# Later fetches, earlier stores and a small planning allowance for first-stage products in a hybrid decoder step whose order a planner writes

## The chip, the cores and the metric

The kernel runs on the 8 cores of one Trainium2 chip. Each core handles one prompt of 2048 tokens and 16 sample tokens, with its own copy of all weights; the cores exchange nothing. The time of an execution is that of its slowest core, in microseconds (us) on the device. The times shown are medians over runs. Engines are named as in the profile: PE (matmul), PEld (its weight loads), DVE (vector), ACT (activation), POOL (GpSimd, which also issues the weight loads on DMA queue q0) and SP (which issues nearly all other transfers, on queue q1).

## The reference, cut to what matters

```python
def layer(x, pool_prev, ...):
    h = rmsnorm(x, g_mix)
    proj = h @ w_in
    a, z = proj[..., :o1], gelu(proj[..., o1:o2])
    gate_a, gate_b = sigmoid(proj[..., o2:o3]), sigmoid(proj[..., o3:])
    pa = pool_mixer(seq_a, ...)              # trailing means of 2, 4, 8, 16 rows, then a 128x128 product
    sg, v = spatial_gating(z, w_s, b_s, g_v) # u * (causal 128x128 mixing of rmsnorm(v) + b_s)
    merged = gate_a * (pa @ w_pool_out) + gate_b * (sg @ w_gmlp_out)
    x = x + merged @ w_out
    h2 = rmsnorm(x, g_ffn)
    x = x + (silu(h2 @ w_gate) * (h2 @ w_up)) @ w_down
    return x, new_pool, v                    # and rmsnorm(x, g_final) is the output
```

Model width is 1024, the FFN has 2816 columns (22 slices of 128), weights arrive as float32 and are cast to float16 by the transfer.

## The kernel before, in words

The program is not written as five instruction streams. Every operation is put on a list by `Prog.add` with an assumed duration, a priority and what it reads and writes, and `Prog.schedule` (L258) plays the list through a model of the five engines, the eight PSUM banks and two DMA queues (`Rings`). Each engine takes next the operation that can start earliest; among equals the one of lowest priority number. The order in which operations were taken is then the order in which each engine issues them on the chip; only the order is kept, not the times. `Prog.resolve` adds the semaphore waits. So an assumed time matters only where it changes an order, and an engine whose next operation is late on the chip stands still though a later one could run.

`slack` is a number added in the model to the moment an operation may start: for a matmul, `schedule` adds it to the moment its operands from other engines are done (L294) and its bank is free (L282). `mm` (L549) gives it 200 ns (`PEM`) for the products after the first stage (priority over 900) and none for those of the first stage. For a DMA the slack is added to its assumed landing.

The stages, in order of time on core 3:

* First stage (to about 121 us): the 16 tiles of 128 rows of x are loaded by SP, normed, transposed on PE (`norm`), and multiplied with the a, v and u parts of w_in. Where the planned order leaves PE idle for over 0.7 us early on, dummy matmuls (L1446) are put in. The row `b_s` is fetched by ACT's queue (`bs_row`, L661) and spread over 128 partitions by a float32 matmul against ones (`spread`, L691).
* Gates and merge (to about 269 us): the gate products in a Strassen-like form with 344 columns (`product`), with weights in three slots `Rg` filled by POOL (`ring_load`, L993: two loads of 256 KB, then four DVE sums on them).
* The product with w_out (to about 331 us): the loop over `wo_order` (L1202), 17 steps n_ = 0 to 16: sixteen tiles of 128 prompt rows, and the 16 sample rows (NT) at n_ = 6. For each prompt tile x is fetched again (`xload`), 16 matmuls of 512 columns fill two banks, DVE adds them to x, ACT and POOL work out the row norm, ACT scales into one of four buffers `hb` (tile `Sx` in the trace), DVE multiplies by the gain, and SP issues a transposing DMA into `hT` (the sample rows are transposed by PE instead). Tiles n_ = 0 to 5 live in `X`; n_ = 7 to 16 in rows 0 to 9 of `Pr`, so they have to be stored to `xd` in DRAM (`xstore`, L1198) before the FFN writes its row f into row f of `Pr`.
* FFN, two groups of 10 and 12 slices: f = 0, 1, 2 run together over the three blocks of 344 columns, then f = 3, 4, 5, 6 one after the other. The weights of f go to slot f % 3 of `Rg`: those of f = 3, 4 and 5 can be fetched only as f = 0, 1 and 2 let their slot go. Then the down projection of each group (`down_pair`), which fetches x from `xd`, adds, and stores it, to `yp` after the last norm.

The orders that the diff touches: the fetches of n_ = 7 to 16 all wait for one thing, that the fetch of prompt tile 10 has landed (`x_dma[10]`). The stores of n_ = 7, 8, 9 follow their own tile's norm; those of n_ = 10 and 11 wait for the last norm of the stage (`tlast`, the landing of its transposing DMA); those of n_ = 12 to 16 wait until the weights of f = 3 have landed (`Bf[3]['ld']`).

Of the kernel before, what the change touches and what calls it, by code (L numbers as in the profile page):

```python
# [34 lines left out]
PEM = 200.0  # L35
# [10 lines left out]
C_BS = 136  # L46
# [386 lines left out]
def nfree(ap):  # L433
    n = 1
    for (_, c) in list(ap.ap)[1:]:
        n *= int(c)
    return n


def build_nc():  # L440
    nc = bass.Bass("TRN2", target_bir_lowering=False, dynamic_dma_scratch_size=4096)

    def din(name, shape):
        return nc.dram_tensor(name, list(shape), F32, kind="ExternalInput").ap()
# [7 lines left out]
    cst = din("cst", [128, C_ALL])  # L452
# [11 lines left out]
    with es:  # L464
# [63 lines left out]
        bs_row = wsb[:, 0:512]  # L528
# [20 lines left out]
        def mm(pt, sl, pairs, prio, start=True, stop=True, after=(), more=False):  # L549
            out = PV(pt, sl)  # L550
            n = nfree(pairs[0][1])
            rd = [x for pr in pairs for x in pr]

            def fn(e):
                ap = P.r(out)
                ins = None
                for i, (l, rr) in enumerate(pairs):
                    ins = e.matmul(out=ap, lhsT=l, rhs=rr, start=(start and i == 0),  # L558
                                   stop=(stop and i == len(pairs) - 1), skip_group_check=more)
                return ins  # L560
            f = 4.0 if pairs[0][1].dtype == F32 else 1.0
            per = max(25.0, n / 2.4 * f + 2.5)
            o_ = P.add('pe', fn, reads=rd, writes=[out], dur=per * len(pairs), lat=140.0, prio=prio, after=after)
            o_.slack = PEM if prio > 900 else 0.0
            return o_

        def pe_multi(pt, items, prio, per, reads, nmm):
# [50 lines left out]
        def rows(n, b):  # L618
            return (max(1.0, n / 16.0), 45.0 + b * 0.04)

        def dma(q, out, in_, sem, nbytes, prio, after=(), tr=False):
            def fn(e):
                if tr:
                    return e.dma_start_transpose(out=out, in_=in_)
                return e.dma_start(out=out, in_=in_)  # L625
            return P.add(q, fn, reads=[in_], writes=[out],
                         dur=(570.0 if q == 'pool' else 450.0), lat=0.0, prio=prio, dma=sem, nbytes=nbytes,
                         after=after, margin=(300.0 if q == 'pool' else 0.0))
# [19 lines left out]
        x_dma = {}  # L648

        def xload(t, prio, after=()):  # L650
            s_ = xtile(t)
            if t < NT:
                o_ = dma('sp', slots[s_][:, 0:D], xp[t * 128:(t + 1) * 128, :], 'x%d' % s_, rows(128, 4096), prio, after)
            else:
                o_ = dma('sp', slots[s_][:NSMP, 0:D], xs[:, :], 'x%d' % s_, rows(16, 4096), prio, after)
            x_dma[t] = o_
# [1 line left out]
        on = memset('dve', ones[0:1, :], 1.0, -9.0)  # L658
        xload(0, -10.0)
        dma('act', idg[:, :], cst[:, C_ID:C_ID + 136], 'c0', rows(128, 544), -9.9)  # L660
        dma('act', bs_row[0:1, :], cst[0:1, C_BS:C_BS + 512], 'c4', rows(1, 2048), -9.8)  # L661
        for t in range(1, NXS):
            xload(t, -10.0 + 0.1 * t)
        wd_ = {}
# [470 lines left out]
        for p in range(4):  # L1135
# [10 lines left out]
            if p == 0:  # L1146
                for k in range(4):
                    load(('wo', k), spare[:, k, :], 'w%d' % (8 + k), 1900.0 + k)
                wo7 = load(('wo', 7), Fr[:, 3952:3952 + 512].bitcast(F16), 'w16', 1903.5)
# [42 lines left out]
        wo_order = [0, 8, 1, 9, 2, 10, NT, 3, 11, 4, 12, 5, 13, 6, 14, 7, 15]  # L1192
# [5 lines left out]
        def xstore(t, prio, o_):  # L1198
            stored[t] = dma('sp', xd[t * 128:(t + 1) * 128, :], slots[xtile(t)][:, 0:D], 'x%d' % xtile(t), rows(128, 4096), prio,
                            after=[o_])  # L1200

        for n_, t in enumerate(wo_order):  # L1202
            pr = 2000.0 + 10.0 * n_
            if t < NT:
                xload(t, 1950.0 + n_, [x_dma[10]] if n_ > 6 else [wo7])
                xv_ = slots[xtile(t)]
                memset('dve', xv_[:, D:D + 1], 32.0 * EPS ** 0.5, pr)
                for h in range(2):
                    pt = PT()
                    pairs = [(merged[:, k, t * 128:(t + 1) * 128], U(('wo', k))[:, h * 512:(h + 1) * 512])  # L1210
                             for k in range(8)]
                    if n_ < 0:
                        mm(pt, lambda p: p[:, :], pairs[:7], 2000.0 + n_, stop=False)
                        mm(pt, lambda p: p[:, :], pairs[7:], pr, start=False)
                    else:
                        mm(pt, lambda p: p[:, :], pairs, pr)
                    xv = xv_[:, h * 512:(h + 1) * 512]
                    vtt(xv, xv, PV(pt, lambda p: p[:, :]), ALU.add, pr, 512)
            else:
                xload(NT, 1950.0 + n_, [wo7])  # L1220
                memset('dve', slots[NXS][:NSMP, D:D + 1], 32.0 * EPS ** 0.5, pr)
                wo_l = [U(('wo', k)) for k in range(8)]
                mg = [merged[:, k, SEQ:TOK] for k in range(8)]
                pv = sample_mm(lambda dd: [(wo_l[k][:, dd * 128:(dd + 1) * 128], mg[k]) for k in range(8)], 8,
                               wo_l + mg, pr)
                act(samT[:, :], pv, AF.Copy, pr, n=128)
                sample_back(samT[:, :], pr)
            tlast = norm(t, gffn, pr + 1.0, t < NT)
            if t < NT and 6 < n_ < 10:
                xstore(t, pr + 100.0, tlast)  # L1230
        for n_, t in enumerate(wo_order):
            if 10 <= n_ < 12:
                xstore(t, 2200.0 + n_, tlast)

        sil0 = table(AF.Silu, sigs)
# [144 lines left out]
        for gi, (f0, nf) in enumerate(groups):  # L1380
            last = gi == 1
            row = (lambda f: f) if gi == 0 else (lambda f: (f - f0 + NFA) % nf)
            fr = {row(f): f for f in range(f0, f0 + nf)}
            flist = list(range(f0, f0 + nf))
            parts = [flist[0:3], flist[3:-3], flist[-3:]] if gi == 0 else [flist[:-3], flist[-3:]]
            Bf = {}
            n_ = 0
            wd = None
            for part in parts:
                bm = part is parts[-1] or (gi == 0 and part is parts[0])  # L1390
                seqn = [(f, j) for j in ((2, 1, 0) if gi == 1 else range(NJ)) for f in part] if bm else [(f, j) for f in part for j in range(NJ)]
                if bm:
                    for f in part:
                        Bf[f] = ffn_load(f, base + 3 * n_)
                for (f, j) in seqn:
                    if gi == 0 and n_ < 9 and f == part[0]:
                        ssum(j, 2990.0 + j, 3500.0)
                    if f not in Bf:
                        Bf[f] = ffn_load(f, base + n_)
                        if gi == 0 and f == 3:  # L1400
                            for i_ in range(12, 17):
                                xstore(wo_order[i_], 2990.0 + i_, Bf[f]['ld'])
                    ffn_unit(row(f), j, Bf[f], base + n_)
                    n_ += 1
                    if n_ == (21 if gi == 0 else 27):
                        raw, B = wd_load(nf, fr, base + 40.0, [Bf[f_]['ld'] for f_ in (range(2, 7) if gi == 0 else range(13, 19))])
            base += 100.0
            hh = nf // 2
            if gi == 0:
                fa = M16[:, 17920:17920 + 1920].rearrange("p (q i c) -> p q i c", q=3, i=5)  # L1410
                fb_ = Fr[:, 3440:3440 + 960].bitcast(F16).rearrange("p (q i c) -> p q i c", q=3, i=5)
                sbufs = [[b_[:, q, :, :] for q in range(3)] for b_ in (fa, fb_)]
            else:
                sbufs = [[hT[:, 0:6, c_:c_ + 128] for c_ in cs] for cs in ((2 * WJ, 2 * WJ + 128, HTOK + 2 * WJ), (WJ, WJ + 128, HTOK + WJ))]
                dma('sp', gfin, cst[:, C_GN:C_GN + 1024], 'c6', rows(128, 4096), base - 60.0)
            if last:
                keep[0] = keep[1]
            for n_, t in enumerate(pair_orders[gi]):
                down_pair(nf, t, B, sbufs[n_ % 2], base + 10.0 * n_, last, gi == 0 and n_ >= 5)
                if n_ == 5:  # L1420
                    down_sample(nf, raw, not last, base + 10.0 * n_ + 5.0)
                    if last:
                        sample_back(samT[:, :], base + 10.0 * n_ + 6.0)
                        final_norm(NT, base + 10.0 * n_ + 7.0)
            base += 100.0
# [7 lines left out]
        for o_ in P.order['pe']:  # L1433
            if o_.start < min(BK7 - 1000.0, 45000.0):
                gap = o_.start - t_
                n_ = int((gap - 700.0) / (430.0 if t_ < 6000.0 else 235.0)) if gap > 700.0 else 0
# [159 lines left out]
```

How the kernel before makes its waits and increments, by code:

```python
    def run(self, eng, e, sems):  # L422
        for o in self.order[eng]:
            for (sk, val) in o.waits:
                e.wait_ge(sems[sk], val)
            ins = o.fn(e)
            if o.dma is not None:
                ins.then_inc(sems[o.dma], 16)
            else:
                ins.then_inc(sems['E_' + eng], 1)
# [1038 lines left out]
            @block.sync  # L1469
            def _(e):
                P.run('sp', e, sems)
                for key in sorted(P.cnt):
                    if key[0] in 'oq':
                        e.wait_ge(sems[key], P.cnt[key])
```

## Time and profile before

| | |
|---|---|
| median of 3 runs | 758.9 us (758.84 to 761.04) |
| the profiled execution | 758.97 us, span of its slowest core (core 3) 756.8 us |
| spans of the cores | 745.9 (core 6) to 756.8 us (core 3) |
| PE busy | 731.1 us, 97% of the span |
| DVE, ACT, POOL busy | 77%, 50%, 14% |
| DMA | 84.05 MB, mean 111 GB/s |

The profile's rows are those of one execution, of its slowest core unless another is named. "Busy" of PE says that a matmul was in the array, at whichever clock it was granted; 1.00 in a PEclk column is 2.4 GHz and 0.50 is 1.2 GHz. The number in square brackets at the end of a timeline row is how long the engine had stood idle, and what it waited for. Time between the span and the execution's own time is 2.2 us, outside the first and last instruction.

### The profile page before, as it was taken

To read this page: it belongs to the slowest core of one execution; us is meant where nothing else is said; L and a number is where in the kernel's file an instruction comes from. 1 tells how busy PE (TensorE), PEld (TensorE's weight loads), DVE (VectorE), ACT (ScalarE), POOL (GpSimd) and SP (SyncE) were. 2 spreads that over 40 slices of the span, in tenths; PEclk is the share of its full clock that TensorE was granted. 3 is DMA by queue.
4 is the path that set the end of the run, shared out by engine and by line. 5 is a ranking of instruction groups with operands and counts; after the bars stand their busy time and mean duration, and the time that the engine had idled before them with its cause. 6 is when DMAs were issued, how large, how long until landed. Compare 5 with 4: busy or idle time off the path is not lost.

```text
span 756.8 us, 15077 instructions; the slowest of 8 cores (745.9 to 756.8 us)
## 1 busy us (share of the span) xinstructions
PE 731.1 (97%) x4771; PEld 431.0 (57%) x4771; DVE 582.9 (77%) x1304; ACT 377.2 (50%) x825; POOL 109.1 (14%) x185
## 2 busy tenths in 40 slices
PE   7999999999999999999979999999999999999995
PEld 3655455666666645456646665455666666654452
DVE  4789999998988885767557667975567776768986
ACT  3586756676766655775525552001555555522232
POOL 5244321000001011110111001000111100002121
PEclk9999999999999999999989999999999999999999
DMA  8997903140313369792994205771356442005762
GB/s 204 242 250 131 142 27 58 15 57 15 57 15 57 115 131 301 190 152 66 173 163 71 42 2 84 221 268 40 59 82 96 73 71 42 2 1 174 227 217 111
DMA packets 50973, 84.05 MB, mean 111 GB/s; under 512 B 24528, under 2 KB 24656, under 8 KB 50880
## 3 DMA queue, kind: packets, MB, share of 16 engines
q0 software_dynamic: 15984, 29.11, 25.9%
q1 hardware_dynamic: 34478, 53.39, 24.6%
q8 instruction: 39, 0.64, 0.4%
q10 hardware_dynamic: 434, 0.60, 0.3%
q14 instruction: 38, 0.31, 0.1%
HBM read 87.90 MB, written 19.49 MB: 142 GB/s over the span
## 4 chain that ended last, share of the span: by engine, by line
PE 82%; DMA 8%; DVE 5%; issue 2%; ACT 1%; SPq 1%; POOL 1%; DVEq 0%; ACTq 0%; POOLq 0%
PE ps L558 80%; DMA Sx<-wpk 3%; DMA Rg<-wpk 3%; DMA hT<-Sx 2%; SPq L625 1%; DVE hT L592 1%; DVE Fr L592 1%; DVE X L600 1%; PE ps L1169 1%; DVE Pr L592 1%; ACT Fr L581 1%; DVE Sx L592 1%; PE ps L742 0%; DVE X L592 0%; POOL Sx L625 0%
## 5 line engine op out<-in xcount | busy, mean ns | idle before, releaser
L581 ACT ACTIVATE Fr<-ps 128x344 f32<-128x344 f32 (+2 forms) x456 | 203.9, 464 | 161.3 <-PE ps L558 131.7
L558 PE MATMUL ps<-hT,Rg 128*128 128x344 f16 x1440 | 247.2, 310 | 0.5
L592 DVE TENSOR_TENSOR Fr<-Fr,ps 128x344 f32<-128x344 f32 (+2 forms) x356 | 175.6, 509 | 68.3 <-ACT Fr L581 42.3
L558 PE MATMUL ps<-Sx,Rg 128*128 128x344 f16 x1080 | 192.4, 310 | 5.6 <-DVE Rg L592 3.9
L558 PEld LDWEIGHTS ps<-hT,Rg 128*128 128x128 f16 x1440 | 140.4, 98 | 73.4 <-issue 3.4
L558 PEld LDWEIGHTS ps<-Sx,Rg 128*128 128x128 f16 x1080 | 104.6, 98 | 60.6 <-issue 9.6
L592 DVE TENSOR_TENSOR X<-X,ps 128x512 f32<-128x512 f32 (+1 forms) x131 | 85.5, 670 | 21.4 <-PE ps L558 19.0
L625 POOL DMA_DIRECT2D Rg<-wpk x60 | 31.8, 531 | 354.4 <-PE ps L558 352.8
L581 ACT ACTIVATE junk<-X 128x1025 f16<-128x1025 f32 (+3 forms) x43 | 44.1, 1024 | 77.0 <-DVE X L592 59.8
L558 PE MATMUL ps<-Mr,Pr 128*128 128x512 f16 x352 | 81.0, 379 | 0.0
L581 ACT ACTIVATE Fr<-Fr 128x344 f16<-128x344 f32 x108 | 52.6, 490 | 55.4 <-DVE Fr L592 55.2
L707 POOL TENSOR_TENSOR rs<-ss,mhalf 128x1 f32<-128x1 f32 (+1 forms) x66 | 47.6, 723 | 207.3 <-ACT junk L581 207.3
L592 DVE TENSOR_TENSOR Pr<-Fr 128x344 f16<-128x344 f16 x132 | 41.6, 334 | 29.9 <-ACT Fr L581 27.3
L558 PE MATMUL ps<-Pr,Mr 128*128 128x512 f16 (+1 forms) x236 | 57.3, 347 | 0.5 <-issue 0.5
L558 PEld LDWEIGHTS ps<-Mr,Pr 128*128 128x128 f16 x352 | 34.2, 98 | 40.4 <-issue 1.1
L592 DVE TENSOR_TENSOR Rg<-Rg 128x512 f16<-128x512 f16 x120 | 47.6, 419 | 7.0 <-DMA Rg<-wpk 5.8
L558 PE MATMUL ps<-Mr 128*128 128x512 f16 (+2 forms) x182 | 46.5, 377 | 2.5 <-DMA Mr<-cst 2.3
L558 PEld LDWEIGHTS ps<-Pr,Mr 128*128 128x128 f16 x236 | 22.6, 98 | 20.3 <-issue 0.8
L558 PE MATMUL ps<-Mr,hT 128*128 128x512 f16 x144 | 33.2, 379 | 0.1
L558 PE MATMUL ps<-hT,Sx 128*128 128x256 f16 (+2 forms) x224 | 30.4, 287 | 2.7 <-DVE hT L592 1.6
L558 PEld LDWEIGHTS ps<-Mr 128*128 128x128 f16 (+2 forms) x182 | 18.4, 108 | 23.6 <-issue 4.6
L558 PE MATMUL ps<-Sx,hT 128*128 128x512 f16 (+1 forms) x136 | 31.1, 379 | 0.3 <-DMA Sx<-wpk 0.2
(133 smaller groups left out, 685.5 us busy)
## 6 DMA issues: line engine op xcount, KB each, us to landing
Rg<-wpk POOLq DMA_DIRECT2D x60, 256.0 KB, 4.0
X<-xp SPq DMA_DIRECT2D x22, 512.0 KB, 15.5
X<-xd SPq DMA_DIRECT2D x18, 512.0 KB, 5.1
Mr<-wpk POOLq DMA_DIRECT2D x33, 256.0 KB, 6.3
yp<-X SPq DMA_DIRECT2D x14, 512.0 KB, 2.9
xd<-Pr SPq DMA_DIRECT2D x12, 512.0 KB, 5.1
Pr<-xp SPq DMA_DIRECT2D x10, 512.0 KB, 11.5
xd<-X SPq DMA_DIRECT2D x8, 512.0 KB, 5.6
```

The source lines that it names most:

```text
L558: ins = e.matmul(out=ap, lhsT=l, rhs=rr, start=(start and i == 0), stop=(stop and i == len(pairs) - 1), skip_group_check=more)
L581: return e.activation(out=P.r(out), in_=P.r(in_), func=func, scale=scale, **kw)
L592: return P.add(eng, lambda e: e.tensor_tensor(out=P.r(out), in0=P.r(a), in1=P.r(b), op=op), reads=[a, b], writes=[out], dur=vdur(n, per), ...
L600: return P.add('dve', lambda e: e.scalar_tensor_tensor(out=P.r(out), in0=P.r(a), scalar=sc, in1=P.r(b), op0=op0, op1=op1), reads=rd, write ...
L625: return e.dma_start(out=out, in_=in_)
L707: P.add('pool', lambda e: e.tensor_tensor(out=rs[:R, k:k + 1], in0=ss[:R, k:k + 1], in1=mhalf[:R, 0:1], op=ALU.pow), reads=[ss[:R, k:k + 1 ...
L1169: ins = e.matmul(out=p[:, dd * 16:(dd + 1) * 16], lhsT=l, rhs=r, start=(i == 0), stop=(i == len(ls) - 1))
```

## The change

Four edits. (1) Matmuls of priority up to 900, those of the first stage among them, get a slack of 100 ns in the planner instead of none. (2) The planner takes the landing of the `b_s` row 3.5 us later than before. (3) In the w_out stage the fetches of n_ = 9 to 16 wait each for the end of the norm seven steps earlier (`tn[n_ - 7]`: the landing of its transposing DMA, for n_ = 13 ACT's copy of the sample rows) instead of all for `x_dma[10]`; those of n_ = 7 and 8 stay. (4) The stores of n_ = 12 to 16 wait for `tlast`, as those of 10 and 11 do, and no longer for the weights of f = 3. No arithmetic is added or removed, and every transfer keeps its size.

```diff
             o_ = P.add('pe', fn, reads=rd, writes=[out], dur=per * len(pairs), lat=140.0, prio=prio, after=after)
-            o_.slack = PEM if prio > 900 else 0.0
+            o_.slack = PEM if prio > 900 else 100.0
             return o_
...
-        dma('act', bs_row[0:1, :], cst[0:1, C_BS:C_BS + 512], 'c4', rows(1, 2048), -9.8)
+        dma('act', bs_row[0:1, :], cst[0:1, C_BS:C_BS + 512], 'c4', rows(1, 2048), -9.8).slack = 3500.0
...
+        tn = []
         for n_, t in enumerate(wo_order):
             pr = 2000.0 + 10.0 * n_
             if t < NT:
-                xload(t, 1950.0 + n_, [x_dma[10]] if n_ > 6 else [wo7])
+                xload(t, 1950.0 + n_, [tn[n_ - 7]] if n_ > 8 else [x_dma[10]] if n_ > 6 else [wo7])
...
             tlast = norm(t, gffn, pr + 1.0, t < NT)
+            tn.append(tlast)
             if t < NT and 6 < n_ < 10:
                 xstore(t, pr + 100.0, tlast)
         for n_, t in enumerate(wo_order):
-            if 10 <= n_ < 12:
+            if 10 <= n_:
                 xstore(t, 2200.0 + n_, tlast)
...
                         Bf[f] = ffn_load(f, base + n_)
-                        if gi == 0 and f == 3:
-                            for i_ in range(12, 17):
-                                xstore(wo_order[i_], 2990.0 + i_, Bf[f]['ld'])
```

## Rows read from the trace of the kernel before

**Rows 1.** Spans and mean granted TensorE clock of three cores.

```profile
core 3: 756.8 us, clock 0.993
core 4: 754.7 us, clock 0.992
core 6: 745.9 us, clock 0.996
```

**Rows 2.** Core 3, timeline, 340 to 390 us: start, length, engine, line, operation.

```profile
342.80 30.48 SPq L625 DMA_DIRECT2D xd<-Pr  x7
365.72 0.54 POOL L625 DMA_DIRECT2D Rg<-wpk  x1 [2.96 <-PE ps L558]
382.99 0.43 DVE L592 TENSOR_TENSOR Rg<-Rg 128x512 f16<-128x512 f16 x1 [5.51 <-DMA Rg<-wpk]
383.56 0.74 PE L558 MATMUL ps<-Sx,Rg 128*128 128x344 f16 x4 [3.91 <-DVE Rg L592]
386.58 2.45 PE L558 MATMUL ps<-Sx,Rg 128*128 128x344 f16 x8 [1.69 <-DVE Fr L592]
```

**Rows 3.** Core 3, SP's waits, 240 to 400 us: us, times, longest.

```profile
SPq L425 <- DMA Rg<-wpk: 25.2, 1, 25.2
```

**Rows 4.** Core 3, windows: length, PE, PEld, DVE, ACT, POOL busy, PEclk, DMA share, GB/s.

```profile
342.00:358.00 16.00, 16.00 (x111) 10.59 (x110) 12.38 (x29) 8.61 (x20) 0.00 (x0) 1.00 0.18 68
...
388.00:389.00 1.00, 1.00 (x5) 0.57 (x4) 0.84 (x2) 0.00 (x0) 0.53 (x1) 0.50 0.80 133
...
391.00:392.00 1.00, 1.00 (x6) 0.53 (x4) 0.89 (x3) 0.84 (x2) 0.00 (x0) 0.57 1.17 152
```

**Rows 5.** Cores 3 and 6, windows 360 to 400 us.

```profile
360.00:400.00 40.00, 34.40 (x218) 21.97 (x217) 20.82 (x55) 16.75 (x38) 6.88 (x13) 0.91 0.90 158
...
360.00:400.00 40.00, 39.37 (x271) 26.24 (x269) 27.32 (x73) 20.28 (x48) 7.97 (x15) 1.00 0.93 177
```

**Rows 6.** Core 3, timeline of the w_out stage.

```profile
276.64 1.15 ACT L581 ACTIVATE Sx<-X,rs 128x1024 f16<-128x1024 f32 x1 [0.80 <-POOL rs L707]
...
279.39 1.91 SPq L624 DMA_TRANSPOSE hT<-Sx  x1
281.41 6.59 SPq L625 DMA_DIRECT2D Pr<-xp  x10
288.11 23.05 SPq L624 DMA_TRANSPOSE hT<-Sx  x7
...
302.77 2.19 ACT L581 ACTIVATE Sx<-X,rs 16x1024 f16<-16x1024 f32 x2 [2.79 <-DMA hT<-Sx]
...
304.85 0.34 PE L742 MATMUL ps<-ident_b,Sx 16*128 16x16 f16 x8 [1.78 <-DVE Sx L592]
305.12 1.04 PE L558 MATMUL ps<-Pr,Mr 128*128 128x512 f16 x4
...
308.58 1.03 PE L558 MATMUL ps<-Pr,Mr 128*128 128x512 f16 x4
```

**Rows 7.** Core 4, PE's timeline, 290 to 420 us: all its waits.

```profile
306.85 0.36 PE L742 MATMUL ps<-ident_b,Sx 16*128 16x16 f16 x8 [4.28 <-DVE Sx L592]
387.06 1.33 PE L558 MATMUL ps<-Sx,Rg 128*128 128x344 f16 x8 [1.69 <-DVE Fr L592]
```

**Rows 8.** Core 4, window 300 to 331 us.

```profile
300.00:331.00 31.00, 26.73 (x120) 11.64 (x119) 17.73 (x27) 18.00 (x24) 3.53 (x8) 0.89 0.71 149
```

**Rows 9.** Core 3, DMA issues: count, KB each, median us from issue to landing.

```profile
Rg<-wpk POOLq DMA_DIRECT2D x60, 256.0 KB, 4.0
...
hT<-Sx SPq DMA_TRANSPOSE x19, 3.7
```

**Rows 10.** Core 3, PE's timeline in the first stage: rows that begin with a wait.

```profile
6.72 2.04 PE L558 MATMUL ps<-Mr 1*128 1x512 f32 x2 [2.29 <-DMA Mr<-cst]
...
19.36 0.61 PE L742 MATMUL ps<-ident_b,Sx 128*128 128x128 f16 x8 [0.47 <-DVE Sx L606]
...
49.51 1.03 PE L558 MATMUL ps<-hT,Sx 128*128 128x256 f16 x8 [0.27 <-ACT Mr L581]
```

## The prediction

> **What bounds the kernel now.** First the spans by core: core 3 sets the time with 756.8 us, core 6 does the same work in 745.9 at nearly the same clock [rows 1]. So 10.9 us of the slowest core are not work that every core must do, and the question is where they lie. PE is busy 97% of the span, so the next views are those of PE standing still. Core 3's timeline has two places after the first stage. Around 380 us, early in the FFN, it stands 3.91 us for sums on `Rg` and 3 us later another 1.69 us for DVE [rows 2]. In the w_out stage it stands 1.78 us for the sample rows' scaled row [rows 6].
>
> What released them: DVE's sum at 382.99 had itself waited for a weight load. By the order of POOL's issues that is the second load of f = 4, issued at 365.72 [rows 2], landing about 17.2 us later where the median load takes 4.0 [rows 9]. In between SP had waited 25.2 us for the weights of f = 3 [rows 3]; seven stores of 512 KB begin at 342.80 and end 30.48 us later [rows 2], and since two went out at once, the other five went out from about 368.8 to 373.3, on top of the weight loads. The stretch from 342 to 358 us, just before, uses 18% of the DMA engines [rows 4].
>
> In the w_out stage ten fetches go out in one piece from 281.41 to 288.0; the transposing DMAs queued behind them let ACT's buffer go only at 302.77, 14.7 us after the issue at 288.11 [rows 6].
>
> **Edit 4, the five stores.** They go to about 343, right behind the two that are there already, on an SP queue that has nothing else to issue until the down projection. Their 2.6 MB then run in the empty stretch. Price of the stall on core 3: 3.91 + 1.69 idle. After it PE runs at 1.2 GHz: eight matmuls take 2.45 us from 386.58 [rows 2] where core 4 needs 1.33 [rows 7]; the clock still reads 0.50 at 388 and averages 0.57 over 391 to 392, that is, full for the last 0.14 us [rows 4]. From 386.58 to 391.86 are 5.28 us at half speed, 2.64 lost. Sum 8.2. Check by counts: core 6 issues 271 matmuls in 39.37 busy us of the same window, 0.145 us each; core 3 issues 218 [rows 5], 53 fewer or 7.7 us, and core 6 itself idles 0.6 there: 8.3. I take 8.2. Without the five stores the load lands after 4.0 us [rows 9], at the worst, if they cost it only half of its 17.2, after 8.6, so at 374.3; four sums of 0.43 us [rows 2] follow, and PE comes to them at 383.56 - 3.91 = 379.65: some 3 us in hand. Late next is what DVE owes then: where the load was in time, on core 6, 0.6 us of idleness remains [rows 5]. I leave 0.4 for that, bounds 0 and 1.7.
>
> By the Trainium skill, "DMA: Bandwidth & Descriptors", section "Queues, rings and completion order", each DMA engine takes queues in turn, packet by packet. Taken alone that halves a load beside stores and speaks against so large a gain: 8 us by twice the row's 4.0, where the row shows 17.2. The row goes beyond the rule, and by the rule some 9 us of the delay would have another cause, which is the third rival below.
>
> **Edit 3, the fetches.** Instead of ten in one piece, two go out at about 281.4 and the others one by one, a step of 3.46 us apart (305.12 to 308.58, [rows 6]). The transposes find one fetch ahead of them, so ACT's buffer is free long before the sample rows need it, and the 1.78 us go. A fetch still has time: let out when the transposing DMA seven steps earlier has landed, it is needed 7 x 3.46 = 24 us after that tile's own product; norm (about 6 us) and landing (3.7, [rows 9]) leave some 14. What is new: SP holds at each of these waits, and behind it stand the next transposing DMA and the stores of n_ = 7 to 9. A step in which SP does nothing else costs 3.7 for the landing and about 0.66 for issuing a fetch (6.59 over ten, [rows 6]): 4.4 us against 3.46, so 0.9 late per step, 7 after the eight. The four buffers allow 4 x 3.46 - 2.75 (copy at 276.64 to transposing DMA at 279.39) - 3.7 = 7.4 us before ACT, then DVE, then PE stand [rows 6, 9]. It just fits, and the planner, which charges a transposing DMA about this much, can put the next one ahead of the fetch. Gain 1.8 here; bounds 4.3 plus the clock's loss (core 4, [rows 7, 8]) and, the other way, the second rival.
>
> The same page, section "Anatomy of one DMA — SWDGE (gpsimd) path", has 2.0 us plus bytes/436e3 per transfer, estimated 2.6 us for a tile of 256 KB: with it a step would be 3.3 us and nothing late. The row's 3.7 is a median of issues that partly stood behind others.
>
> **Edits 1 and 2, the first stage.** The `b_s` row is waited for 2.29 us, and the spread then takes 2.04 [rows 10], but the first tile's transposes at 10.39 wait for x in any case: the spread moves behind them into time now filled by dummies. Worth nothing; if it meets a product, up to 2.0 lost. The 100 ns can only reorder. What they can recover is the idleness between 19.36 and 49.51: seven waits, from 0.47 to 0.27, together 2.8 us [rows 10], partly waits for x that no order removes. A bad order could cost as much. I take 0.3 gained, bounds 2.8 either way.
>
> **Sum.** Core 3: 756.8 - 8.2 - 1.8 + 0.4 - 0.3 = 746.9. The others, freed of the same two places, must not stay above: core 4 loses 4.28 + 1.69 idle [rows 7] and, by a mean clock of 0.89 over 31 us, 6.8 us at half speed, 3.4 lost [rows 8]: 754.7 - 9.4 = 745.3. Core 6 is at 745.9 already. So core 3 stays the slowest, at 746.9; the profiled execution lies 2.2 us above its span (758.97 to 756.8) and within 0.1 of the median. Hence 749.1; the skew between cores being as it may, 749.0.
>
> **Rivals.**
> *The w_out stall stays on some core* (fetches late or SP holding, no worse than now). Then core 4 sets the time with only 1.69 gone: 753.0, with the 2.2 755.2. For it: its size differs much between cores 3 and 4 [rows 6, 7], so it hangs on more than the order, and the eight waits on SP are new. Against: ten fetches ahead of a transposing DMA become one.
> *Slower: SP serialises the stage.* If each landing also includes the fetch ahead (ten took from 281.4 to 302.8, 2.1 us each, [rows 6]), a step costs 6.5 us, 3.0 too many, 24 over eight steps; less 7.4 of buffers that is 17 of PE idleness against 10 gained: 766. It decides from a step of 3.46 + (7.4 + 10)/8 = 5.6 us up. For it: the transposing DMAs have taken 14.7 us behind fetches. Against: a step in which the next transposing DMA goes first loses nothing.
> *The stores do not matter.* If the load of f = 4 was held 17.2 us by something other than the five stores, the 8.2 stay: 756.8 - 1.8 + 2.2 = 757.2, no measurable change. For it: if stores cost a load half of its time, 8.6 us of the 17.2 are left unexplained. Against: the median load, beside no stores, takes 4.0 us [rows 9], and core 6 idles only 0.6 us there [rows 5], so nothing in the loads' own order makes them late.
> *The first stage gets worse by 2 to 4 us* through a new order: 751 to 753.
>
> **How the numbers follow.** Forecast as summed, 0.70 (746.5 to 751); first stage worse 0.08; w_out stall stays 0.11; stores without effect 0.06; serialised 0.05. A change of 0.3% (2.3 us) is about what a measurement tells from none, so faster is under 756.6: the first three, 0.89. Same: 0.06. Slower: 0.05. The range runs from 746.0 (most of the first stage's 2.8 recovered) to 754.0, which takes in the fourth rival and the lower part of the first, and leaves some 0.18 outside.
>
> **What would show it.** Right: seven stores in a row at about 342 us, the second load of f = 4 landing in under 7 us, no wait of PE on `Rg`, PEclk 1.00 from 360 to 400 us; fetches of `Pr` spread from 281 to 320 us; no wait before the sample rows' transposes; spans within 3 us of each other. Wrong: a new wait of PE in the w_out stage behind DVE, with ACT waiting for `hT`; idleness in the first stage above its 2.8 us.

## The result, and the profile after

The changed kernel takes 748.95 us (median of 6 runs), the kernel before 759.63 us on the same chip: ratio 0.9861, 95% interval 0.9843 to 0.988. The forecast was 749.0 us, range 746.0 to 754.0. The profiled execution of the changed kernel took 748.58 us, its slowest core (now core 2) 746.9 us. Ratios leave out executions in which the cores of one die were granted a lower clock; the last repeat of the changed kernel (below) has its profile from such an execution, so of that profile only cores 4 to 7, the other die, are used.

The spans by core answer to [rows 1]. Three of the eight, the two ends among them:

```profile
core 0: 745.4 us, clock 0.993
core 2: 746.9 us, clock 0.990
core 6: 745.9 us, clock 0.997
```

Core 6, which had been free of most of the waiting, needs what it needed before, 745.9 us. The others came down to it: 745.4 to 746.9 us instead of 749.3 to 756.8. Work was not made faster; waiting that only some cores had in full was removed.

Core 2's queues around the places of [rows 2, 3], as the timelines of SP and POOL, and DVE's sums of f = 4:

```profile
341.87 6.61 SPq L625 DMA_DIRECT2D xd<-Pr  x7
...
364.74 0.54 POOL L625 DMA_DIRECT2D Rg<-wpk  x1 [2.37 <-PE ps L558]
365.90 0.53 POOL L625 DMA_DIRECT2D Rg<-wpk  x1 [0.62 <-PE ps L558]
367.31 1.07 POOL L625 DMA_DIRECT2D Mr<-wpk  x2 [0.87 <-DMA Rg<-wpk]
...
371.49 1.62 DVE L592 TENSOR_TENSOR Rg<-Rg 128x512 f16<-128x512 f16 x4
```

All seven stores go out in one run at 342 us. DVE's four sums at 371.49 begin with no wait in brackets: their loads were there (the second load of f = 4, issued at 364.74, landed 5.2 us later). The windows answer to [rows 4, 5] and to the window of the w_out stage in [rows 8]:

```profile
0.00:20.00 20.00, 13.62 (x78) 8.16 (x79) 8.50 (x20) 7.75 (x15) 9.67 (x22) 0.74 0.88 204
...
300.00:331.00 31.00, 31.00 (x155) 14.27 (x153) 20.99 (x32) 21.76 (x30) 6.50 (x12) 1.00 0.94 225
...
360.00:400.00 40.00, 40.00 (x276) 26.81 (x275) 28.20 (x76) 20.92 (x50) 9.03 (x17) 1.00 0.74 113
```

From 300 to 331 and from 360 to 400 us PE is busy without a gap at full clock. No core of this execution shows a wait of PE between 290 and 420 us. The first 20 us have become worse: a granted clock of 0.74, where core 3 of the kernel before reads 1.00:

```profile
0.00:20.00 20.00, 14.02 (x91) 6.85 (x92) 8.44 (x20) 7.81 (x15) 9.66 (x22) 1.00 0.87 206
```

The fetches of `Pr` and what SP waits for, core 2, 282 to 320 us (in [rows 6] the ten fetches were one piece):

```profile
282.26 0.98 SPq L625 DMA_DIRECT2D Pr<-xp  x2
...
289.97 0.34 SPq L625 DMA_DIRECT2D Pr<-xp  x1
...
304.38 0.33 SPq L625 DMA_DIRECT2D Pr<-xp  x1
...
315.46 0.33 SPq L625 DMA_DIRECT2D Pr<-xp  x1
...
318.56 0.78 SPq L625 DMA_DIRECT2D Pr<-xp  x1
```
```profile
SPq L425 <- DMA hT<-Sx: 14.0, 6, 3.3
```

SP does hold for landings, as the second rival said: six times between 278 and 340 us, 14.0 us in all, 3.3 at most. It costs nothing in this execution, since PE has no wait.

In the first stage three new waits stand in PE's timeline (core 2), answering to [rows 10], and a long one before the first transposes:

```profile
9.94 1.01 PE L742 MATMUL ps<-ident_b,Sx 128*128 128x128 f16 x8 [3.89 <-DVE Sx L606]
...
69.81 0.59 PE L558 MATMUL ps<-Mr 128*128 128x512 f16 x2 [0.51 <-DVE Mr L606]
71.02 0.60 PE L959 MATMUL ps<-idg,aTs 128*16 128x128 f32 x4 [0.62 <-ACT Pr L581]
80.65 0.65 PE L558 MATMUL ps<-Mr 128*128 128x512 f16 x2 [0.40 <-DVE Mr L611]
```

### The profile page after: what moved, and what is told of

It is laid out like the page before. It is cut to its first block, busy times and chain, and to the rows that moved or that the text cites. A ratio compares the mean times of both kernels' runs of the same rounds, so it can differ in the third digit from the quotient of the medians.

```text
span 746.9 us, 15081 instructions; the slowest of 8 cores (745.4 to 746.9 us)
## 1 busy us (share of the span) xinstructions
PE 728.1 (97%) x4767; PEld 431.9 (58%) x4767; DVE 583.0 (78%) x1304; ACT 377.2 (50%) x825; POOL 107.9 (14%) x185
## 4 chain that ended last, share of the span: by engine, by line
PE 92%; DMA 3%; DVE 2%; issue 1%; POOL 0%; ACT 0%; DVEq 0%; ACTq 0%; POOLq 0%
PE ps L558 90%; DMA Sx<-wpk 3%; PE ps L1169 1%; DVE X L600 1%; DVE hT L592 1%; PE ps L742 0%; POOL Sx L625 0%; PE ps L901 0%; ACT Mr L581 0%; PE ps L1184 0%; DVE ps L600 0%; DVE Pr L592 0%; PE ps L881 0%; DVE Mr L606 0%; DVEq L1467 0%
## 5 line engine op out<-in xcount | busy, mean ns | idle before, releaser
L592 DVE TENSOR_TENSOR Fr<-Fr,ps 128x344 f16<-128x344 f32 (+2 forms) x356 | 175.9, 509 | 63.2 <-ACT Fr L581 39.5
```

The lines of the kernel that those rows point to most:

```text
L592: return P.add(eng, lambda e: e.tensor_tensor(out=P.r(out), in0=P.r(a), in1=P.r(b), op=op), reads=[a, b], writes=[out], dur=vdur(n, per), ...
```

## The experiments

Two summaries are used throughout; both are worked out from the profiled execution of each kernel as means over its eight cores (`full_third`: over four). Each is one execution, and single cores lie up to 5 us from their mean. "First" runs from PE's first transposes to ACT's table load for the gates, "w_out" on to the first FFN product, "FFN" to the end of the span (the gates are in "w_out"). The last three columns are PE's idleness in the w_out stage (290 to 320 us), at the seam to the FFN (320 to 345) and in the early FFN (345 to 420).

```
                       ratio to before           first  w_out   FFN   idle: w_out seam FFN
before                                           112.5  209.9  420.8        2.6  0.0  2.4
e12_slack              1.0016 [1.0006, 1.0027]   114.5  210.6  421.4        3.0  0.0  2.9
e4_stores              0.9924 [0.9905, 0.9943]   112.9  210.1  418.2        2.5  0.0  0.7
e3_fetches             0.9878 [0.9863, 0.9893]   113.1  206.3  418.8        0.0  0.2  0.7
e34_no_slack           0.9874 [0.9857, 0.9891]   113.2  206.6  418.6        0.2  1.2  0.1
changed kernel         0.9861 [0.9843, 0.9880]   113.7  206.1  417.2        0.0  0.0  0.0
full_again             0.9895 [0.9863, 0.9926]   114.2  206.1  417.6        0.0  0.4  0.0
e341_no_late_row       0.9873 [0.9852, 0.9895]   114.3  206.1  418.6        0.0  1.1  0.0
e342_no_100ns          0.9886 [0.9855, 0.9918]   113.8  206.4  417.8        0.1  0.5  0.1
pm34_after_product     0.9875 [0.9857, 0.9893]   112.9  206.3  418.8        0.0  0.0  1.3
wd_late                0.9950 [0.9932, 0.9969]   112.8  209.8  419.3        2.6  0.0  1.6
tn4_fetch_late         0.9943 [0.9920, 0.9965]   113.0  206.3  425.2        0.0  4.1  1.4
pm34_wd_late           0.9874 [0.9858, 0.9889]   113.1  206.2  418.5        0.0  0.0  0.7
full_third, cores 4-7  0.9895 [0.9866, 0.9925]   114.3  206.3  418.4        0.2  1.2  0.0
```

**Each part alone.** `e4_stores` is edit 4 without the rest:

```diff
-            if 10 <= n_ < 12:
+            if 10 <= n_:
                 xstore(t, 2200.0 + n_, tlast)
...
-                        if gi == 0 and f == 3:
-                            for i_ in range(12, 17):
-                                xstore(wo_order[i_], 2990.0 + i_, Bf[f]['ld'])
```

> Edit 4 alone (stores of n_ 12 to 16 at the end of the w_out stage). Theory: the wait on Rg early in the FFN is gone on every core (8.2 us on the core that lost most), the wait before the sample rows' transposes stays at 1 to 4 us, with a low clock after it on some cores: the slowest core is then one like core 4 of before with only its 1.7 us gone, 755 us in all. Rival, stores without effect on the loads: 759 and the wait on Rg still there.

Ratio 0.9924. The early FFN's idleness falls from 2.4 to 0.7 us on the mean, and no PE wait on `Rg` is left on any core; the w_out wait stays (2.5). The stores matter.

`e3_fetches` is edit 3 without the rest:

```diff
+        tn = []
...
-                xload(t, 1950.0 + n_, [x_dma[10]] if n_ > 6 else [wo7])
+                xload(t, 1950.0 + n_, [tn[n_ - 7]] if n_ > 8 else [x_dma[10]] if n_ > 6 else [wo7])
...
+            tn.append(tlast)
```

> Edit 3 alone (fetches one by one). Theory: no wait before the sample rows' transposes, the wait on Rg and the low clock after it stay on some cores: about 757 us, 0.3% under before. Rival, that the two stalls hang together (a core late in the w_out stage meets the stores at another place): the wait on Rg changes too, up to all of it gone, 750, or grown, 760 or more.

Ratio 0.9878: alone it gives nearly all of the gain. The w_out wait goes, as forecast, but the FFN wait at 380 us goes too, though all five stores are still let out by the same landing (0.7 us of idleness remains, nearly all of it after 390 us). The prediction had no place for that. This run's own rival had it, by another path (a core meeting the stores at another place); the POOL order shows what changed. First the kernel before, core 3: the two rows of the chain of waits that hold these loads (start, length, what), and POOL's timeline behind the first load of f = 5, the one at 365.72 in [rows 2].

```profile
362.24 6.60 DMA Rg<-wpk
370.08 12.74 DMA Rg<-wpk
```
```profile
369.48 0.53 POOL L625 DMA_DIRECT2D Mr<-wpk  x1 [3.21 <-PE ps L558]
370.08 0.53 POOL L625 DMA_DIRECT2D Rg<-wpk  x1
370.62 0.53 POOL L625 DMA_DIRECT2D Mr<-wpk  x1
```

The load that DVE waits for at 382.99 went out at 370.08, not at 365.72: it lands 12.74 us later, at 382.82. The one at 365.72 is the first load of f = 5. Between the two stands a load of w_down (tile `Mr`), for which POOL stood still 3.21 us: in the program it waits for the weights of f = 3, those issued at 362.24 and 6.60 us under way. (The bracket names PE, on which POOL waits there too; the landing comes at 368.84, and the issue 0.64 us behind it.) The same landing lets SP issue the five stores, from 368.90. So POOL, held in order by a load that belongs to the down projection, much later, issued the urgent load 1.2 us behind the first of five stores. Now `e3_fetches`, core 3, POOL and then SP:

```profile
362.78 0.54 POOL L625 DMA_DIRECT2D Rg<-wpk  x1 [2.38 <-PE ps L558]
363.95 0.53 POOL L625 DMA_DIRECT2D Rg<-wpk  x1 [0.62 <-PE ps L558]
365.24 1.06 POOL L625 DMA_DIRECT2D Mr<-wpk  x2 [0.76 <-DMA Rg<-wpk]
369.19 1.05 POOL L625 DMA_DIRECT2D Mr<-wpk  x2 [2.89 <-DMA Rg<-wpk]
370.23 0.55 POOL L625 DMA_DIRECT2D Rg<-wpk  x1
...
364.66 3.45 SPq L625 DMA_DIRECT2D xd<-Pr  x5
```

With edit 3 the planner writes another order for POOL (its model's times in the w_out stage have shifted): the second load of f = 4 (362.78) now precedes the first of f = 5 and the w_down loads, 1.9 us ahead of the stores. What stands behind them is the second load of f = 5 (370.23), which is not needed before some 387 us.

`e34_no_slack` is both together:

> Edits 3 and 4 (fetches and stores) without edits 1 and 2 (planning of the first stage). Theory: the two moved transfers hold the whole gain, and the new order of the first stage costs 1 us, since in the profile after the stretch from the first tile's transposes to the start of the gates is 1.2 us longer in the mean of the cores (113.7 against 112.5): this kernel takes about 748.0 us, 1.0 under the changed one, with no wait of PE in the w_out stage or early in the FFN. Rival, as predicted: the first-stage edits gain 0.3, so this takes about 749.3.

0.9874, as edit 3 alone: the two gains overlap, and the theory (748.0 us, no wait of PE) failed. The idleness is in a new place, at the seam to the FFN, 1.8 to 2.8 us on each of cores 0 to 3. PE on core 1, and what SP waits for there from 278 to 345 us:

```profile
339.24 0.74 PE L558 MATMUL ps<-Sx,Rg 128*128 128x344 f16 x4 [2.19 <-ACT Fr L581]
```
```profile
SPq L425 <- DMA hT<-Sx: 19.0, 7, 5.1
```

PE waits for ACT, ACT for DVE, and DVE at 333.65 had waited 2.36 us for a transposing DMA. This is the second rival at a small part of its price: 2.19 us here, where it gave 17.

`e12_slack` is edits 1 and 2 alone:

```diff
-            o_.slack = PEM if prio > 900 else 0.0
+            o_.slack = PEM if prio > 900 else 100.0
...
-        dma('act', bs_row[0:1, :], cst[0:1, C_BS:C_BS + 512], 'c4', rows(1, 2048), -9.8)
+        dma('act', bs_row[0:1, :], cst[0:1, C_BS:C_BS + 512], 'c4', rows(1, 2048), -9.8).slack = 3500.0
```

> Edits 1 and 2 alone (planning of the first stage). Theory: the first stage is 1 us longer and both later stalls stay: 760.5 us, 1 over before. Rival, as predicted: 0.3 gained, 759.3. Either way below what 0.3% can tell; the stretch from the first tile's transposes to the gates' table load, core by core, says more: 113.7 in the mean by the theory, 112.5 or less by the rival.

1.0016, an interval just above 1. The first stage takes 114.5 us; in the kernel before and the seven others that leave it as it was it takes 112.5 to 113.2. By themselves the two edits cost time, as the theory had it.

**The first stage, one edit at a time, on top of edits 3 and 4.** `full_again` repeats the changed kernel beside `e341_no_late_row` (without the 3500) and `e342_no_100ns` (without the 100).

> The changed kernel itself, as the control beside its parts on one chip. Theory (edits 1 and 2 cost about 1 us in the first stage; the rest of the order is that of edits 3 and 4 alone): ratio to before 0.986, and the two kernels with one of the first-stage edits left out are under it. Rival (the first-stage edits are worth 1 to 2 us, as the ratios 0.9861 and 0.9874 from two chips would have it): it is the fastest of the three.

> The changed kernel without edit 2 (landing of the b_s row). The 100 ns order brings three waits between 68 and 80 us, 1.5 us together, and takes away about 1 us between 36 and 50: by the theory that edit 1 costs little and edit 2, whose spread comes after the first tile's transposes and leaves PE idle and at 1.2 GHz in front of them, costs most of the 1.2 us, this takes 0.8 us less than the changed kernel. Rival, edit 1 is the one that costs: the same time as the changed kernel, within 0.4 us.

> The changed kernel without edit 1 (100 ns). Theory (edit 2 costs most): as the changed kernel within 0.5 us, the stretch from the first transposes to the gates' table load 113.3 us or more in the mean of the cores. Rival (edit 1 costs): 0.8 us less than the changed kernel and that stretch at 112.7 or less.

The three ratios (0.9895, 0.9873, 0.9886) can't be told apart. The profiles tell more. From the first transposes to the run of 48 matmuls near 21 us, mean over the cores, the eight kernels with neither edit take 11.3 to 11.6 us, edit 1 alone 11.8, edit 2 alone 12.1, both 11.9 (the changed kernel), 12.0 (`full_again`) and 12.1 (`e12_slack`). From there to the table load it is 101.1 to 101.8 with neither, 102.5 with edit 1, 101.7 with edit 2, 101.9, 102.1 and 102.4 with both. So edit 2 alone costs some 0.5 us in the first 20, and beside edit 1 at most 0.3: with the spread no longer ahead of the first transposes PE stands idle there, 1.3 to 3.9 us on the cores of the changed kernel where it was 0.2 to 0.9, and afterwards runs slower for longer. On core 2 the granted clock is 0.74 over these 20 us, and eight matmuls of one shape still take 1.01 us at 15.59 (core 2), where core 3 before took 0.61 at 15.64:

```profile
15.59 1.01 PE L558 MATMUL ps<-hT,Sx 128*128 128x128 f16 x8 [0.20 <-DVE hT L592]
```

Edit 1 costs up to 1 us, but not in the waits of 69 to 81 us shown above. These are on all cores (from 60 to 90 us PE idles 1.6 to 1.8 us on the mean with edit 1, 0.3 to 0.4 without), but from 22 to 60 us it idles less, 0.8 to 1.2 instead of 1.4 to 1.9. Over the whole first stage PE's idleness is 4.1 to 4.7 us with neither edit and 3.9 to 4.7 with one or both. What grows is its busy time: 108.4 to 108.8 us with neither, 109.5 to 110.3 with one or both. The granted clock from 10 to 20 us is 1.00 on every core of the eight kernels with neither edit, and lower on four cores of eight with edit 1 alone and on all eight with edit 2 alone. The clock is thus the likely cause of the loss; that it is the whole of it isn't shown, since the dummies between the products change as well. Neither theory of the two runs holds as it stands: with either edit left out the stage still takes 113.8 to 114.3 us.

**No hold of SP.** `pm34_after_product` has edit 4, and lets each fetch wait for DVE's product that feeds the transposing DMA, seven steps earlier, instead of that DMA's landing:

```diff
+                if n_ > 8:
+                    xload(t, 2001.5 + 10.0 * (n_ - 7), [mul[n_ - 7]])
```

> Edits 3 and 4 in another form, without 1 and 2: the fetches of n_ 9 to 16 wait for DVE's multiplication of the norm seven steps earlier, and are ordered right behind its transposing DMA, so that SP never holds for a landing. Theory: what made two cores wait about 2 us for hT at the start of the FFN in the kernel with edits 3 and 4 alone is SP holding behind landings, so transposing DMAs go out sooner here, that wait is gone on all cores, and the time is 748 us, 1 under the changed kernel. Rival: the transposing DMAs are late because the DMA engines are full, and a fetch queued ahead of each costs as much as SP's waits: no difference beyond 1 us, and the wait for hT stays.

0.9875, as `e34_no_slack`, and not the 748 us of the theory. SP's waits for landings fall from 15 to 19 us (`e34_no_slack`) to 3.3 (core 1; SP waits 17.5 us for DVE's products there), and the seam's idleness is gone on all eight cores, as the theory had it. But the planner's POOL order is that of before, the w_down load ahead of the second load of f = 4, and 1.3 us of idleness return in the FFN. One hold went, the other came back.

**POOL's hold by itself.** `wd_late` has none of the four edits. Only one pair of w_down loads, those at 369.48 and 370.62 above, waits in the program for f = 4 instead of f = 3:

```diff
-    [Bf[f_]['ld'] for f_ in (range(2, 7) if gi == 0 else range(13, 19))]
+    [Bf[f_]['ld'] for f_ in ((2, 4, 4, 5, 6) if gi == 0 else range(13, 19))]
```

> None of the four edits; only the w_down loads of row 1 wait in the planner for the weights of f = 4 instead of f = 3, which puts the second load of f = 4 (and that of f = 5) ahead of them in POOL's order; the five stores stay where they were, after the landing of f = 3. Theory now (the load of f = 4 was late because POOL, held by a w_down load until f = 3 had landed, issued it behind the stores that the same landing let out): it is issued within 5 us of the first load of f = 5, before 368 us, lands in 4 to 8 us, PE does not wait for sums on Rg at 370 to 395 us on any core, and the w_out wait stays as it was; time 0.990 to 0.995 of before, as with edit 4 alone. Rival, the stores as such: whatever is in flight beside them is late, so a wait of 3 us or more on Rg stays on some core and the time is 0.997 to 1.002. Rival, the 256 KB loads are slow in any order: as the former, with the landing at 10 us or more though it was issued ahead of the stores.

0.995, idleness 1.6 instead of 2.4: between the two theories. The load goes out 1.2 us behind the first of f = 5, as planned, but only 0.1 to 1.0 us ahead of the stores. On six cores the sums begin 5.4 to 8.1 us after its issue, on two 9.0 and 10.8, and there PE waits 2.00 and 3.77 us. Core 7, from POOL's issue over SP's stores and DVE's first sum to PE:

```profile
367.99 0.53 POOL L625 DMA_DIRECT2D Rg<-wpk  x1 [0.62 <-PE ps L558]
...
368.10 3.75 SPq L625 DMA_DIRECT2D xd<-Pr  x5
...
378.80 0.95 DVE L592 TENSOR_TENSOR Rg<-Rg 128x512 f16<-128x512 f16 x2 [5.97 <-DMA Rg<-wpk]
...
380.44 1.31 PE L558 MATMUL ps<-Sx,Rg 128*128 128x344 f16 x4 [3.77 <-DVE Fr L592]
```

So both count, the order on POOL and the stores. Kernels with both causes, one, or neither make a square. From the issue of the second load of f = 4 to its landing in the trace, mean over eight cores (and range):

```
                           stores after f = 3       stores at 342 us
POOL held (order before)   11.2 (9.3 to 13.4)       6.3 (5.0 to 7.4)    before      | e4_stores
load ahead of w_down        7.5 (5.2 to 10.6)       4.8 (4.2 to 5.5)    wd_late     | pm34_wd_late
```

Moving the stores alone takes 43% off, changing POOL's order alone a third, both together 57%. `pm34_wd_late` also lets its fetches out by another rule; a pair with the same fetches is `e3_fetches`, where the load goes out 1.9 to 2.6 us ahead of the stores, 6.0 (5.7 to 6.5), and `e34_no_slack`, with the stores at the end of the w_out stage, 5.3 (4.8 to 5.9).

**The margin of a fetch.** `tn4_fetch_late` is `e34_no_slack` with the fetches let out three steps (10.4 us) later:

```diff
-                xload(t, 1950.0 + n_, [tn[n_ - 7]] if n_ > 8 else ...
+                xload(t, 1950.0 + n_, [tn[n_ - 4]] if n_ > 8 else ...
```

> Edits 3 and 4 with the fetch of n_ waiting for the norm four steps earlier instead of seven, that is 10.4 us later. The prediction's margin (24 us from the releasing landing's own product to the need, of which 14 to spare): still some 3.5 us to spare, so no wait of PE for sums on the fetched tile; time as edits 3 and 4, 0.986 to 0.990. Rival, SP holding at each landing and the landings being slow (the prediction's serialisation): a fetch then comes after its need, PE waits behind DVE in the w_out stage on most cores, 3 to 20 us in all, time 0.992 to 1.012.

0.9943: some 5 us worse than with seven steps (0.0069 of 760, from two chips), as the rival had it; the theory and its margin failed. On core 4 DVE waits for fetched tiles, and PE then for DVE and ACT, 4.1 us at the seam on the mean of the cores. Another 1.4 are in the FFN, where the planner's POOL order has fallen back to that of before. DVE's waits from 300 to 345 us, and three of PE's:

```profile
DVE Pr L592 <- DMA Pr<-xp: 14.1, 4, 4.3
```
```profile
330.69 0.74 PE L558 MATMUL ps<-hT,Rg 128*128 128x344 f16 x4 [0.72 <-DVE Pr L592]
333.48 0.74 PE L558 MATMUL ps<-Sx,Rg 128*128 128x344 f16 x4 [2.04 <-ACT Fr L581]
...
336.14 1.30 PE L558 MATMUL ps<-Sx,Rg 128*128 128x344 f16 x4 [1.33 <-DVE Pr L592]
```

**Neither hold.** `pm34_wd_late` is `pm34_after_product` with the change of `wd_late`, beside `full_third`, the changed kernel once more.

> Fetches held by the product seven steps earlier and not by a landing (no wait of SP for a transposing DMA), stores as in edit 4, and the w_down loads of row 1 behind the weights of f = 4 in POOL's order: neither queue holds a load for another's landing. If what is left above the work common to all cores are those holds: no wait of PE after 290 us on any core, where one of the two alone still had 0.5 to 1.8 us, and 0.5 to 2 us less than the changed kernel, 0.984 to 0.988. Rival: spans are already set by the work common to all cores, and the remaining waits lie on cores that do not set the time; then equal to the changed kernel within 0.2%.

> The changed kernel once more, beside the run with neither hold on the same chip: 0.986 to 0.990 of before.

0.9874 and 0.9895, intervals that overlap. Idleness at the seam is gone, but 0.7 us remains in the FFN (up to 1.6 on one core), where the theory had no wait on any core; the spans are 745.8 to 748.5 us. The time lies in the theory's range too, so the rival is not proved, only not excluded. There is no version here that is shown to beat the changed kernel.

## Why the prediction came out

The time was right to 0.1 us, and that close it is luck: errors of size cancel, and the two repeats on other chips gave 0.9895, some 8 us gained, where the forecast had 9.9 and the first measurement 10.7. Span of the slowest core, stage by stage: core 3 before, core 2 after. Start to the first transposes, 10.39 and 9.94; first stage 112.38 and 113.88; w_out 208.26 and 206.01; FFN 425.77 and 417.07.

**What bounds it: right.** The signs named for a right forecast are all there: the seven stores, the load's first use within 6.8 us of its issue (364.74 to 371.49), the spread fetches, no wait on `Rg` or ahead of the sample rows. One sign of being wrong is there too, more idleness in the first stage (3.89 us ahead of the first transposes on core 2). The 10.9 us between cores 3 and 6 were stalls, and without them all cores stand within 1.0 us of core 6's old span.

**Edit 4: the size right, the path to it wrong at one step.** 7.8 net was forecast (8.2 less 0.4 owed by DVE), 8.7 came in the FFN, with nothing owed. It is not edit 4's alone: on the mean of the cores the FFN takes 2.6 us less with edit 4, 2.0 with edit 3 and 3.6 with the whole change, so either edit takes away much of the same stall. The price stood on PE's idleness and clock, which were read rightly. The step that failed is "the second load of f = 4, issued at 365.72, landing about 17.2 us later": it was issued at 370.08 and took 12.7, and it was late twice, held behind a w_down load and then put behind stores. The third rival's argument against itself, "nothing in the loads' own order makes them late", was wrong, and its count of 8.6 us "unexplained" was a right sign: 4.4 of the 17.2 are another load's. The stores' own part, 4.8 us of landing in the upper row of the square, 2.6 in the lower, is what edit 4 takes away. By the Trainium skill, "DMA: Bandwidth & Descriptors", section "Queues, rings and completion order", engines take queues in turn, packet by packet; the prediction took from it that stores at most double a load. The means of the square agree, 1.8 times in the upper row and 1.5 in the lower; one core of `wd_late`, at 10.6, is at 2.2 times the 4.8. The 17.2 that had seemed to go beyond the rule was not one load's time, and the 4.0 beside it is the median of all loads: this one takes 6.3 without the stores, with other loads of its own queue under way.

**Edit 3: gain right, margin wrong, and it does more than was said.** 1.8 was forecast for core 3, 2.25 came; on the mean of the cores 3.8 (209.9 to 206.1). The margin of "some 14" us is about 3 where it is least: on core 2 the last fetch is issued at 318.56 and lands 6.7 us later, at 325.30, and DVE's sums on it begin at 328.44, so 3.1 us are left; the seven others that edit 3 lets out have 4.6 to 10.2. The sum had counted one landing of 3.7 where the loop has two (5.1 for a transposing DMA after the change, 4.8 for a fetch, medians), and nothing for standing in SP's queue. With 10.4 us taken off, late fetches follow, though the waits of `tn4_fetch_late` on core 4, up to 4.3 us, are smaller than 10.4 less 3.1. The 2.6 us per transfer that the prediction estimated by the Trainium skill, "DMA: Bandwidth & Descriptors", section "Anatomy of one DMA — SWDGE (gpsimd) path", is stated there for transfers issued by POOL, and the transposing DMAs are SP's. The case agrees with it in neither: the transposing DMAs take 5.1 us, and POOL's own loads of 256 KB 4.0 [rows 9], at the median.

SP's holds were forecast as 0.9 us per step and within the buffers; 14.0 us in six waits, and no wait of PE in this execution, bear it out. In other executions they do reach PE, at the seam: on cores 0 to 3 of `e34_no_slack`, and in the changed kernel itself with 2.6 us on core 7 of `full_again` and 2.6 and 2.2 us on cores 5 and 7 of `full_third`, whose spans are 750.0 to 750.3 us beside 746.4 and 746.9 on cores 4 and 6 of `full_third`. So the second rival, at a small part of its price, is in the changed kernel too, and the first profile happened to be free of it. What decides between executions isn't settled; without the holds (`pm34_after_product`, `pm34_wd_late`) the seam has no wait on any core.

That edit 3 alone removes the FFN stall at 380 us was not foreseen. It is shown as a fact; that it comes by the reordered POOL queue is supported by its issue times and by `wd_late`, where an order of the same kind without edit 3 takes away a third of the idleness.

**Edits 1 and 2: wrong sign.** 0.3 gained was forecast, with 2.8 either way; core to core the first stage lost 1.5, by its mean 1.2, and 2.0 in `e12_slack` (0.8 and 1.6 against 112.9, the mean of the eight kernels that leave the first stage as it was). The spread did move behind the first transposes, into time that dummies had filled; the step that failed is that this is "worth nothing": ahead of the transposes the spread had kept PE going, and its removal left 3.89 us idle and the products up to some 18 us at the lower clock (core 2). Of the idleness between 19.36 and 49.51 the 100 ns did recover some (0.6 us on the mean from 22 to 60), and the new waits from 69 to 81 took it back. The forecast had named a loss only where the spread meets a product.

**The sum.** -7.8 - 1.8 - 0.3 was forecast, -9.9; measured -8.7 - 2.25 + 1.5 and -0.45 before the first transposes, -9.9. The first stage's loss was paid by the other terms; the -0.45 was in no term of the forecast, and it compares two cores of which the first transposes begin anywhere from 8.0 to 10.5 us (mean 9.1 after, 9.5 before).

## What to carry to other kernels

An urgent load is as late as whatever stands ahead of it on its issuing engine, and a wait there, on something nobody needs yet, is as good as a longer transfer: read the queue's order by what each issue is for, not by its tile's name. With an order written by a planner an edit at one place can reorder another engine 40 us later, so take the parts of a change one at a time and compare the queues before giving the credit. A fetch that waits for a landing has two landings in its loop; count both before spending the margin.

## What the runs showed of the hardware that had not been expected

- A 256 KB load issued ahead of five 512 KB stores by 0.1 to 1.0 us is still slowed: it lands after 7.5 us on the mean, up to 10.6 (`wd_late`), against 4.8 without them (`pm34_wd_late`). Issued 1.9 to 2.6 us ahead it takes 6.0 (`e3_fetches`) against 5.3 (`e34_no_slack`). Being issued first does not protect it; a longer lead helps.
- With the 2.0 us of the spread gone from ahead of the first transposes, PE stands idle there for 1.3 to 3.9 us, and the granted clock behind them is lower: from 10 to 20 us 0.57 to 0.83 on seven of the eight cores of the changed kernel (0.57 on core 2), where all eight cores read 1.00 before.
